# Twelve weight differences of the state-space scan made by GpSimd in place of VectorE, around its first rotations

## What is computed

```python
def ssd_dilated_layer(x, ...):
    h = rms_norm(x, norm_w)
    proj = jnp.einsum("bsd,df->bsf", h, w_in)     # z, xbc, dt, q, k, v, g
    ...
    # scan over 16 heads (ssd_chunked_scan), three groups of attention on q, k, v
    # whose q and k are rms-normed and rotated (partial_rope)
```

## Time and profile before

| | us |
|---|---|
| median of 3 runs | 1670.7 (1670.03 to 1671.16) |
| span of the profiled execution, first to last instruction | 1666.9 |
| the runs' median less that span | 3.8 |
| PE busy | 1564.8 (94%) |
| DVE busy | 486.1 (29%) |
| ACT busy | 267.3 (16%) |
| POOL busy | 73.5 (4%) |
| mean granted clock of PE | 0.991 of full |

### The profile page before, as it was taken

One profiled execution on the slowest core, in us unless ns is written; L12 is line 12 of the kernel. 1 busy time (PEld: TensorE's weight loads), 2 busy tenths in 40 slices (PEclk: granted clock), 3 DMA queues, 4 the chain that ended last, 5 costly groups with the idle time before them and its releaser, 6 DMA issues. The chain is left out here.

```text
span 1666.9 us, 25063 instructions
## 1 busy us (share of the span) xinstructions
PE 1564.8 (94%) x10674; PEld 1038.9 (62%) x10674; DVE 486.1 (29%) x932; ACT 267.3 (16%) x667; POOL 73.5 (4%) x138
## 2 busy tenths in 40 slices
PE   9999999998989899999999998898999899999998
PEld 8855555555555576465556555554888678758874
DVE  4941000000000313440000000002436897346642
ACT  1020000000000112210000000001132233321331
POOL 0000000000000000000000000000000432001220
PEclk9999999999999899999999999999999999999999
DMA  9689999999999942499999999999233224233420
GB/s 389 268 320 370 429 426 429 427 428 428 428 428 427 398 151 101 181 420 412 428 428 428 429 428 428 428 427 423 109 131 122 102 102 151 102 116 137 152 101 26
DMA packets 38519, 502.52 MB, mean 301 GB/s; under 512 B 4272, under 2 KB 4528, under 8 KB 6064
## 3 DMA queue, kind: packets, MB, share of 16 engines
q1 hardware_dynamic: 37872, 499.40, 72.8%
q0 software_dynamic: 576, 2.10, 0.3%
HBM read 500.43 MB, written 1.05 MB: 301 GB/s over the span
## 5 line engine op out<-in xcount | busy, mean ns | idle before, releaser
L854 PE MATMUL ps<-x_tok,tables_sb 128*128 128x256 f32 x1228 | 305.1, 392 | 0.0
L854 PEld LDWEIGHTS ps<-x_tok,tables_sb 128*128 128x128 f32 x1228 | 220.9, 189 | 102.8 <-issue 77.1
L877 PE MATMUL ps<-ring,arena 128*32 128x256 f32 x3968 | 238.6, 382 | 30.2 <-DMA ring<-in_expert_up 20.5
L877 PEld LDWEIGHTS ps<-ring,arena 128*32 128x32 f32 x3968 | 118.5, 109 | 139.2 <-issue 31.0
L719 PE MATMUL ps<-spare,ring 128*128 128x256 f32 x768 | 169.7, 383 | 0.9 <-DVE spare L2121 0.9
L2357 DVE TENSOR_TENSOR arena<-arena,ps 128x128 f32<-128x128 f32 x64 | 18.4, 288 | 497.0 <-ACT arena L1723 497.0
L719 PEld LDWEIGHTS ps<-spare,ring 128*128 128x128 f32 x768 | 147.3, 192 | 22.3 <-DVE spare L2121 1.2
L940 PE MATMUL ps<-ring,arena 128*32 128x512 f32 x928 | 115.0, 612 | 16.4 <-ACT arena L1718 11.3
L1303 PE MATMUL ps<-ring 128*128 128x256 f32 x480 | 110.5, 383 | 1.4 <-ACT tables_sb L1851 1.3
L751 PE MATMUL ps<-ring,arena 128*128 128x512 f32 x224 | 98.7, 595 | 2.9 <-ACT arena L1841 1.3
L1303 PEld LDWEIGHTS ps<-ring 128*128 128x128 f32 x480 | 89.5, 190 | 18.7 <-issue 6.9
(11 more groups left out here) (299 smaller groups left out, 1396.3 us busy)
## 6 DMA issues: line engine op xcount, KB each, us to landing
ring<-in_expert_up SPq DMA_DIRECT2D x124, 2048.0 KB, 20.4
ring<-in_stream SPq DMA_DIRECT2D x43, 2048.0 KB, 8.2
ring<-in_expert_down SPq DMA_DIRECT2D x42, 2048.0 KB, 24.1
ring<-in_expert_down SPq DMA_DIRECT2D x32, 1024.0 KB, 22.3
arena<-in_expert_up SPq DMA_DIRECT2D x4, 2048.0 KB, 11.2
arena<-in_expert_down SPq DMA_DIRECT2D x2, 2048.0 KB, 12.4
tables_sb<-in_expert_down SPq DMA_DIRECT2D x2, 2048.0 KB, 9.9
spare<-in_expert_down SPq DMA_DIRECT2D x2, 2048.0 KB, 10.2
```

The costliest lines, as they stand in the source:

```text
L854: pe.matmul(ps[:, b, 0:TOK], ident, x[:, 0, 0:TOK], start=True, stop=True, skip_group_check=True)
L877: ins = pe.matmul(ps[q * SLOTS:(q + 1) * SLOTS, 4 + e % 2, 0:TOK] .rearrange("p (g n) -> p g n", g=2), xg[:, 4 * half + k, e * SLOTS:(e + ...
```

## The change

Differences 0 to 11, those of chunks 6, 7 and 8 of the SSD layer, are taken from DVE and made by POOL with the same operation on the same tiles. POOL makes 0 to 7 first, then rotates q of group 0, then makes 8 to 11, then rotates k of group 0. They count on a semaphore of their own, `scan_sums`, for which PE waits in the products of these three chunks; later differences stay on DVE and `w_sums` counts from 0 at the thirteenth. Because POOL may reach them before the expert layer is over, it waits for the last expert chunk ahead of the first one.

```diff
--- before.py
+++ after.py
@@ -168,6 +168,7 @@
     sevens = [base[stage] + n for stage, which in ((SSD, range(6, 15)), (MOBA, (0, 1, 2, 4, 5, 6)))
               if stage in on for n in which]
     seven_no = {g: c for c, g in enumerate(sevens)}
+    scanned = 3 if SSD in on else 0
     late = min([base[stage] for stage in (SSD, MOBA) if stage in on], default=at)
     place_of, loads_of, before_in = {}, {}, {}
     held, loaded = {}, [0] * RING
@@ -626,11 +627,11 @@
         def _(pool):
             step = Steps(pool, "pool_step")
 
-            def rotate(grp, gains):
+            def rotate(grp, gains, which=range(2)):
 
 
                 mul = ALU.mult
-                for w in range(2):
+                for w in which:
                     pool.wait_ge(sem("head_y"), 2 * grp + w + 1)
 
                     v, y, u = head_v[:, w], head_y[:, w], head_w[:, w]
@@ -662,6 +663,28 @@
                     step.settle()
                     pool.sem_inc(sem("at_qk"), 1)
 
+            def scan_sums(which):
+
+
+                for n in which:
+                    c, q = divmod(n, 4)
+                    w = slot8[slot(sevens[c])]
+                    if q == 0:
+                        arrive(pool, sevens[c])
+                    if MOE1 in on and n == 0:
+                        pool.wait_ge(chunk_done, base[SSD])
+                    if n >= W_SUMS:
+                        c6, q6 = divmod(n - W_SUMS, 4)
+                        pool.wait_ge(sem("product"), 6 * c6 + FREED_AT[q6])
+                    if q in (1, 3):
+                        pool.wait_ge(sem("scan_sums"), n if q == 1 else n - 1)
+                    w11, w12, w21, w22 = (w[:, 4 * a_:4 * a_ + 4, TOK * b_:TOK * b_ + TOK]
+                                          for a_ in range(2) for b_ in range(2))
+                    a_, b_ = ((w12, w11), (w22, w_sum[(n - 1) % W_SUMS]), (w22, w12),
+                              (w21, w_sum[(n - 2) % W_SUMS]))[q]
+                    pool.tensor_tensor(w_sum[n % W_SUMS], a_, b_, ALU.subtract)\
+                        .then_inc(sem("scan_sums"), 1)
+
             pool.wait_ge(const_in, 32)
             for n, stage in enumerate(on):
                 if stage in (CONV, STICK):
@@ -676,7 +699,10 @@
                 if stage == SSD:
                     if first < SSD:
                         pool.wait_ge(sem("late_in"), 16 * ((first == CONV) + (first < STICK) + 1))
-                    rotate(0, gains)
+                    scan_sums(range(8))
+                    rotate(0, gains, (0,))
+                    scan_sums(range(8, 12))
+                    rotate(0, gains, (1,))
                     rotate(1, gains)
                     rotate(2, gains)
                 if stage == MOBA:
@@ -1285,7 +1311,11 @@
                 if n in (2, 3, 5):
                     pe.wait_ge(sem("kept"), 3 * c + (2, 3, 5).index(n) + 1)
                 if n in (1, 2, 4, 6):
-                    pe.wait_ge(sem("w_sums"), 4 * c + (1, 2, 4, 6).index(n) + 1)
+                    done = 4 * c + (1, 2, 4, 6).index(n) + 1
+                    if c < scanned:
+                        pe.wait_ge(sem("scan_sums"), done)
+                    else:
+                        pe.wait_ge(sem("w_sums"), done - 4 * scanned)
                 if n == 6:
                     pe.wait_ge(sem("added"), added_no(g))
                 low, high, left, right = slice(0, 4), slice(4, 8), slice(0, TOK), slice(TOK, 512)
@@ -2613,7 +2643,7 @@
             def w_sums(upto):
 
 
-                for n in range(summed[0], min(upto, 4 * len(sevens))):
+                for n in range(max(summed[0], 4 * scanned), min(upto, 4 * len(sevens))):
                     summed[0] = n + 1
                     c, q = divmod(n, 4)
                     w = slot8[slot(sevens[c])]
@@ -2626,7 +2656,7 @@
                         else:
                             dve.wait_ge(sem("product"), 6 * c6 + FREED_AT[q6])
                     if q in (1, 3):
-                        dve.wait_ge(sem("w_sums"), n if q == 1 else n - 1)
+                        dve.wait_ge(sem("w_sums"), n - 4 * scanned - (q == 3))
                     w11, w12, w21, w22 = (w[:, 4 * a_:4 * a_ + 4, TOK * b_:TOK * b_ + TOK]
                                           for a_ in range(2) for b_ in range(2))
                     a_, b_ = ((w12, w11), (w22, w_sum[(n - 1) % W_SUMS]), (w22, w12),
```

## The result

The changed kernel takes 1679.8 us (median of 4 runs, 1679.05 to 1681.47) against 1670.4 for the kernel before (4 runs): a ratio of 1.0057, interval 1.0041 to 1.0072, so slower by 0.6%. Measured once more later, beside other kernels, it was 1683.3 us against 1670.95, ratio 1.0074, interval 1.0054 to 1.0093. The span of its profiled execution is 1678.5 us, 11.6 above the span before. The forecast was a span of 1678.7 and a time of 1682.5.

What follows compares the result with a forecast made beforehand. PE, busy 94% of the span, bounds the kernel. Wait 11.5 + low clock 2.5 - given back 2.2 = 11.8 us; span 1666.9 becomes 1678.7, plus 3.8 gives 1682.5 us. Own range 1680 to 1684.5; 8 in 10, 1677 to 1686.

Steps and rivals of the forecast that it cites:

- rival (a): After PE's wait DVE catches up for good, so the late idle and its low clock go, 4.9 us: 1677.6; chance 0.12.
- Relief of DVE: DVE loses twelve operations, 14.6 us, between 1247.3 and 1281.7 us, where PE waits for nothing: worth 0 us.
- Differences 0 to 7 at no cost: On POOL, idle since 574 us, they are ready near 1247 and 1262 us, before the scan's products need them: 0 us.
- The stand: PE idles 11.5 us ahead of product 1 of chunk 8, from 1298.47 us until POOL's difference 8 at 1310.0.
- one difference: One such subtraction on POOL takes 2.0 us, about twice its 128x512 operation of 1.04; ends 1.22 and 2.8.
- the rotation's end: POOL's rotation of q, ahead of difference 8, ends at 1308.0 us, 1308.22 in the trace before.
- The low clock: PE resumes after its new wait at 1.2 GHz, costing 2.5 us, with ends 1.5 and 5.0.
- Given back: While PE waits, DVE and ACT finish what they are behind with, so later PE idles go: 2.2 us together.
- The idle on ACT: PE's 1.34 us ahead of product 3, waiting for an ACT copy held behind a square of `gated(3)`, goes.
- the idle ahead of the sum: PE's 0.22 us of idle ahead of the sum that needs DVE's decay of head 10 goes.
- the 0.64 us within it: The sum on PE needing DVE's decay of head 10 takes its usual 0.70 us in place of 1.34.
- The 2.70 us ahead of `y(7)`: PE's late idle stays, its DVE chain from `y(4)` taking 10.7 us as before, and the clock loss after it stays.

Runs made afterwards that it cites:

- twelve first: Changed kernel with POOL making all twelve differences ahead of the rotation of q; ratio 1.0012 to the kernel before (1.0000 to 1.0024).
- earlier on DVE: Kernel before, all differences on DVE, with 12 to 15 moved earlier in DVE's order; ratio 0.9981 to the kernel before (0.9968 to 0.9994).
- busy stand: Changed kernel with 24 matmuls on PE ahead of the waiting product 1 of chunk 8; ratio 1.0057 to the kernel before.
- wait alone: Kernel before, all differences on DVE, with PE made to wait for the rotation of q ahead of product 1 of chunk 8; ratio 1.0073.
- sixteen first: Changed kernel with differences 0 to 15 all on POOL, ahead of the rotation of q; ratio 0.9980 to the kernel before (0.9968 to 0.9992).

## Why the prediction was right

Its mechanism held at each step, and its range of 8 in 10 (1677 to 1686) held the time. The narrower range of the forecast itself, 1680 to 1684.5, missed 1679.8 by 0.2 us, and 1679.8 lies nearer to rival (a), 1677.6, than to 1682.5: it is the trace, not the time, that tells them apart.

- Relief of DVE priced at 0: twelve first shows it, with the idles of 1.34 and 2.70 us as in the earlier trace rows. What gained was to take differences 12 to 15 from where DVE is full (earlier on DVE).
- Differences 0 to 7 at no cost: POOL made them by 1263.7 us, and PE is full until 1299.
- The stand: 11.5 forecast, 11.65 measured. The term mis-sized in it is one difference, 2.35 us for 2.0. I had doubled an operation of 512 words which reads one operand by broadcast; the estimate of 2.25 us, half of the Trainium skill's figure from "GPSIMD Engine Reference", section 3.1, was nearer, and the trace's 2.35 decides. That the stand came out within 0.15 us is in part luck, for errors cancel: with the scan 0.57 us later in this trace, and taking that off, the rotation's end at 1308.10 is 1307.53 on the scale of before, for which I had 1308.0, so 0.5 less; the operation adds 0.35, and hand-overs that I had left out 0.3 (0.18 from the rotation to the difference, 0.13 from the difference to PE).
- The low clock: 2.5 forecast; 3.75 - 1.99 = 1.76 for the product and 0.15 for the sums, 1.9 us. That it is the clock, busy stand shows.
- Given back: 2.2 forecast. The idle on ACT, the idle ahead of the sum and the 0.64 us within it are gone. The 2.70 us ahead of `y(7)` stay: from the end of `y(4)` to `y(7)` run 1330.91 - 1320.18 = 10.73 us, as before to the hundredth. So rival (a) is out, and busy stand and wait alone show the same 2.70.
- The sum within the stretch: 11.65 + 1.9 - 2.2 = 11.35, against 10.98 measured; 0.13 of the difference is the late product (3.35 for 3.48); most of the rest is that product 3, now right behind product 2, saves 1.58 us for an idle of 1.34. Against the 11.8 us forecast the stretch is 0.8 us short; the 0.6 us more ahead of the scan, which I had not forecast, cover most of that, so that the spans agree to 0.2 us is luck too.
- What was off is the time, 1682.5 for 1679.8. I added 3.8 us, the difference between the runs' median and the span of one execution. In every execution on record 1.7 to 2.1 us lie around the span, so half of the 3.8 says that the traced execution before was quicker than its median; the changed kernel's traced one (1680.38 us at a span of 1678.5) was not. With 1.9 the forecast would have been 1680.6, but that only compares it with the execution traced. From median to median I forecast 11.8 us more; the runs showed 9.5 (6.8 to 12.0) and then 12.4 (9.0 to 15.5). Both intervals hold 11.8, and why the first came out at 9.5 stays open.

## What to carry to other kernels

Work given to an idle engine costs by its place in that engine's order: ask what the engine waits for ahead of it, and when the first reader comes. Here four subtractions stood behind a wait that ends at 1297.8 us and a rotation of 10.4 us, and their reader came at 1298.5; that cost 11 us, while all twelve ahead of that wait cost 0.4 us by the trace and 2.0 (0.0 to 4.0) by the runs. And what a busy engine is relieved of counts only where the bounding engine waits for it: moving four operations of 1.2 us within DVE's own order gained 3.6 us by the trace and 3.2 (1.0 to 5.3) by the runs; taking twelve off it where PE was full gained none.

## What the runs showed of the hardware

GpSimd's operation holds up VectorE's operations with two SBUF inputs, at most for about as long as it lasts: one of 128x256 takes 1.66 us in place of 0.42 beside GpSimd's of 2.40 (twelve first), and 2.60 us where it starts at 1286.51, right behind one of GpSimd's at 1286.48 (sixteen first). VectorE's in turn hold GpSimd's: its operation on 128x16 words takes 1.25 us beside VectorE's differences of 1.28 and 0.22 where VectorE reads PSUM. The Trainium skill's page "GPSIMD Engine Reference", section 8 "Key points", names this contention for VectorE's operations with two SBUF inputs; the traces agree and give its size. After an idle of 2.70 us on PE the low clock costs more or less from one execution to the next: the same product takes 2.71 to 3.75 us, and the changed kernel's two traces differ by 1.1 us in the stretch.
